# Expert results added into x by float32 products with zeros and ones, instead of a scatter to DRAM and a reload

## The reference

```python
def run_block(args):
    tok, e, wt = args
    xb = h[tok]
    y = (jax.nn.silu(xb @ w_g[e]) * (xb @ w_u[e])) @ w_d[e]
    return y.astype(jnp.float32) * wt[:, None]

ys = lax.map(run_block, (row_tok..., block_e, row_w...))
out = jnp.zeros((T, D), jnp.float32).at[row_tok].add(ys.reshape(P, D))
...
x = x_mid + g2 * f[:B * N].reshape(B, N, D)
return rmsnorm(x, final_norm)
```

## Time and profile before

| | us |
|---|---|
| runs | 1578.85, 1578.13, 1573.48 |
| median | 1578.13 |
| the profiled execution | 1576.79 |
| its span, first to last instruction | 1575.0 |
| TensorE busy | 1398.2 (89%) |
| VectorE busy | 724.6 (46%) |
| ScalarE busy | 415.5 (26%) |
| mean granted TensorE clock | 0.962 |

### The profile page before, as it was taken

How to read it: one execution, slowest core, us unless ns; L and a number is a source line. 1 busy time by engine, 2 the same in 40 slices (tenths; PEclk the granted TensorE clock), 3 DMA queues, 4 the chain that set the end, 5 groups by cost and what they waited for, 6 DMA issues and landing times.

```text
span 1575.0 us, 16738 instructions
## 1 busy us (share of the span) xinstructions
PE 1398.2 (89%) x6766; PEld 964.7 (61%) x6766; DVE 724.6 (46%) x1190; ACT 415.5 (26%) x585; POOL 49.1 (3%) x78
## 2 busy tenths in 40 slices
PE   6999999999949998778889785999896999999995
PEld 5889778787833432223233223788675888888883
DVE  5899977767322110001001004767668425343346
ACT  4522234463320000000000003423325314132323
POOL 0000000000000000100000100000000000000000
PEclk9999999999979999999999998999997999999997
DMA  9341343443678999999999997331011332332301
GB/s 368 116 161 54 127 160 134 163 163 98 276 298 343 426 426 428 426 426 427 427 426 426 426 415 258 101 121 54 28 53 54 107 107 82 105 103 83 107 0 54
DMA packets 116708, 336.88 MB, mean 214 GB/s; under 512 B 6824, under 2 KB 74536, under 8 KB 91168
## 3 DMA queue, kind: packets, MB, share of 16 engines
q1 hardware_dynamic: 109488, 316.82, 51.5%
q0 software_dynamic: 6576, 17.01, 3.0%
q10 hardware_dynamic: 576, 2.10, 0.3%
HBM read 331.42 MB, written 13.13 MB: 219 GB/s over the span
## 4 chain that ended last, share of the span: by engine, by line
PE 41%; SPq 18%; DMA 6%; DVE 5%; issue 1%; ACT 1%; ACTq 0%; DVEq 0%; POOLq 0%
SPq L1350 17%; PE second_bank L2504 10%; PE second_bank L2505 9%; PE second_bank L2506 9%; PE moe_bank L1704 5%; PE moe_bank L1716 3%; DMA moe_weights<-in_w_exp_down_dram 2%; DMA vals<-in_w_exp_down_dram 2%; PE second_bank L2638 1%; PE second_bank L2613 1%; DMA kq<-y_dram 1%; DVE x_mid L2417 1%; DMA work<-h_rows_dram,moe_tok_i 1%; DVE x_mid L2420 0%; PE second_bank L2621 0%
## 5 line engine op out<-in xcount | busy, mean ns | idle before, releaser
L1704 PE MATMUL moe_bank<-moe_weights,work 128*64 128x512 f32 x528 | 128.7, 639 | 35.6 <-DMA moe_weights<-in_w_exp_up_dram 22.5
L2504 PE MATMUL second_bank<-second_cx_lo,second_c_hi 128*128 128x512 f32 x352 | 140.2, 398 | 13.2 <-DVE second_cx_lo L2175 9.9
L1621 DVE TENSOR_TENSOR work<-moe_bank,work 128x512 f32<-128x512 f32 x17 | 11.8, 692 | 295.2 <-PE moe_bank L1704 295.2
L2505 PE MATMUL second_bank<-second_cx_hi,second_c_lo 128*128 128x512 f32 x352 | 138.1, 392 | 0.0
L2506 PE MATMUL second_bank<-second_cx_hi,second_c_hi 128*128 128x512 f32 x352 | 138.0, 392 | 0.0
L978 PE MATMUL mixer_bank<-mixer_h_lo,mixer_w_hi 128*128 128x512 f32 x320 | 131.8, 412 | 0.7 <-DVE mixer_w_lo L611 0.4
L2504 PE MATMUL second_bank<-g_lo,second_c_hi 128*128 128x512 f32 x320 | 127.9, 400 | 1.2 <-DVE g_lo L2322 1.2
L979 PE MATMUL mixer_bank<-mixer_h_hi,mixer_w_lo 128*128 128x512 f32 x320 | 126.6, 396 | 0.0
L980 PE MATMUL mixer_bank<-mixer_h_hi,mixer_w_hi 128*128 128x512 f32 x320 | 126.5, 395 | 0.0
L2505 PE MATMUL second_bank<-g_hi,second_c_lo 128*128 128x512 f32 x320 | 125.1, 391 | 0.0
L2506 PE MATMUL second_bank<-g_hi,second_c_hi 128*128 128x512 f32 x320 | 125.0, 391 | 0.0
(11 more groups left out here) (421 smaller groups left out, 2264.2 us busy)
## 6 DMA issues: line engine op xcount, KB each, us to landing
moe_weights<-in_w_exp_down_dram SPq DMA_DIRECT2D x20, 2048.0 KB, 33.6
moe_weights<-in_w_exp_gate_dram SPq DMA_DIRECT2D x17, 2048.0 KB, 33.2
moe_weights<-in_w_exp_up_dram SPq DMA_DIRECT2D x16, 2048.0 KB, 33.5
second_c_raw<-in_w_mlp_dram SPq DMA_DIRECT2D x32, 1024.0 KB, 5.0
mixer_raw<-in_w_in_dram SPq DMA_DIRECT2D x18, 1024.0 KB, 5.3
mixer_raw<-in_w_mod_t_dram SPq DMA_DIRECT2D x16, 1024.0 KB, 4.8
spare<-in_w_exp_up_dram SPq DMA_DIRECT2D x6, 2048.0 KB, 32.6
kq<-in_w_exp_down_dram SPq DMA_DIRECT2D x6, 2048.0 KB, 33.3
```

The lines of the kernel that those rows point to most:

```text
L1704: ins = pe.matmul(out[m * e:m * e + m, :], x_t[:, c, m * e:m * e + m], parts[:, e, k, :], start=(c == 0), stop=(c == KC - 1))
L2504: pe.matmul(out, a_hi, b_lo, start=first, stop=False)
L2505: pe.matmul(out, a_lo, b_hi, start=False, stop=False)
```

## The change

The scatter, the DRAM tensor `y`, its reload, and the gating, adding and transposing at the head of the second stage are removed. In their place:

- ScalarE and VectorE multiply a pair's result by the gate of each slot while they copy it into `y_rows`.
- VectorE writes for each pair a matrix of 128 slots by 512 tokens, one where a slot holds a token (`token_one`, from `iota_row`, now 512 wide).
- TensorE multiplies, for each of the 8 chunks of 128 features, `y_rows` (128 slots by 128 features) with `token_one`: 8 products of 128 x 128 by 128 x 512 (`results`), unsplit float32. They stand between parts 1 and 2 of the next pair; those of the last pair stand at the end. They go through banks 0, 1, 4 and 5.
- VectorE adds each of the 8 outputs, times `g2`, into `x_mid` (`added`).
- The gates are computed at the start of the stage, and two small lists bring them to the slots (`gate_list`, `slot_gates`, and the late ones with `late_list`).
- Six instead of four weight slots are filled from the mixer stage. Slot 4 is the memory of the mixer's `raw` buffers and is filled once the last low part is made; slot 5 is that of `w_hi[0]` and `w_lo[0]` and is filled when the last unit but one of the mixer is computed.
- GpSimd clears `x_rows` once before the first gather.

```diff
-EARLY = 4
+EARLY = 6
...
             sp.wait_ge(mlo_done, KC)
             for n in range(EARLY):
+                if n == 4:
+                    sp.wait_ge(lo_done, NS)
+                if n == 5:
+                    sp.wait_ge(acc_ready, first_tile[NS - 1])
                 first_experts(n)
...
-            sp.wait_ge(scattered, 16 * n_late + 16 * BLOCKS + 16)
-            for t in range(TC):
-                for k, rows in enumerate((vals, kq)):
-                    sp.dma_start(rows[:, 1024 * t:1024 * t + 1024],
-                                 dram["y"][...]).then_inc(y_landed[t], 16)
...
+            pool.wait_ge(xst_ready, 2 * TC)
+            step(pool.memset(x_rows, 0.0))
             pool.wait_ge(h2_stored, 16 * TC)
             pool.wait_ge(first_rows_ready, 1)
             gather_rows(tok_i[:, 0:1])
...
-                pool.wait_ge(y_low, b + 1)
-                pool.wait_ge(y_high, b + 1)
-                scatter_rows(row_i[:, b:b + 1])
...
-                act_e.wait_ge(scattered, 16 * no + 16)
-                act_e.activation(y_rows[:, 0:512], bank[6][:], ACT.Copy).then_inc(y_low, 1)
+                if at[1] is not None:
+                    act_e.wait_ge(late_columns, at[1] + 1)
+                elif at[0] == 0:
+                    act_e.wait_ge(slot_gates_ready, 1)
+                if at[1] is not None or at[0]:
+                    act_e.wait_ge(f_ready, 8 * no)
+                act_e.activation(y_rows[:, 0:512], bank[6][:], ACT.Identity, scale=gate_column(at)).then_inc(y_first, 1)
...
-            def y_second(at):
+            def second_half(at):
                 dve.wait_ge(*done(at, 5))
-                dve.wait_ge(scattered, 16 * turn_no(at) + 16)
-                dve.tensor_copy(y_rows[:, 512:1024], bank[7][:]).then_inc(y_high, 1)
+                dve.tensor_scalar(y_rows[:, 512:1024], bank[7][:], gate_column(at), None, ALU.mult).then_inc(y_second, 1)
+
+            def added(no):
+                if not isinstance(no, int) or no:
+                    dve.wait_ge(f_used, 8 * no)
+                for c in range(KC):
+                    dve.wait_ge(f_ready, 8 * no + (c + 1))
+                    dve.scalar_tensor_tensor(out=x_mid[:, c, :], in0=bank[F_BANK[c % 4]][:],
+                                             scalar=mod_col[:, 40 + c:41 + c], in1=x_mid[:, c, :],
+                                             op0=ALU.mult, op1=ALU.add).then_inc(f_used, 1)
+
+            def chosen_tokens(at):
+                dve.tensor_scalar(token_one, iota_row[:], token_column(at), None, ALU.is_equal).then_inc(one_ready, 1)
...
             for b in range(BEFORE):
+                if b == 2:
+                    late_lists()
+                if b:
+                    added(b - 1)
+                chosen_tokens((b, None, None))
                 if b == 1:
                     late_slots()
                 gated((b, None, None))
                 if b + 1 < BEFORE:
                     x_shifted((b + 1, None, None))
-                if b == 2:
-                    late_lists()
-                    token_gates()
-                y_second((b, None, None))
+                if b == 0:
+                    slot_gates()
+                second_half((b, None, None))
...
+            def results(no):
+                pe.wait_ge(y_first, no + 1)
+                pe.wait_ge(y_second, no + 1)
+                pe.wait_ge(one_ready, no + 1)
+                for c in range(KC):
+                    if c >= 4:
+                        pe.wait_ge(f_used, 8 * no + (c - 3))
+                    out = bank[F_BANK[c % 4]][:]
+                    pe.matmul(out, y_rows[:, 128 * c:128 * c + 128], token_one, start=True, stop=True)\
+                      .then_inc(f_ready, 1)
...
                     if j < 2:
                         pe.wait_ge(x_done, 2 * no + (j + 1))
+                    if j == 2 and (i is not None or b):
+                        ...
+                        results(b - 1 if i is None and n_late is None else ...)
                     if j == 4:
+                        if i is not None or b:
+                            pe.wait_ge(f_used, 8 * no)
                         before_down()
                         pe.wait_ge(a_done, no + 1)
-                        if i is not None or b:
-                            pe.wait_ge(y_low, no)
-                            pe.wait_ge(y_high, no)
...
                     transpose_act((b, None, None))
+                    if b == 0:
+                        gate_list()
                     if b == 1:
                         late_list()
...
+            results(n_late + (BLOCKS - 1))
...
             act.wait_ge(in_landed, 16)
             act.activation(w_hi[0][:], first_raw, ACT.Copy).then_inc(hi_done, 1)
-            for t in range(TC):
-                act.wait_ge(y_landed[t], 32)
-                act.activation(f_rows[:, t, :], f_rows[:, t, :], ACT.Identity, scale=gates[:, t, 0:1])\
-                   .then_inc(f0_ready, 1)
-            act.wait_ge(side_landed, 32)
-            act.activation(wf_hi[:], w_forget[:], ACT.Copy).then_inc(wfhi_done, 1)
             for c in range(KC):
-                act.wait_ge(xf_ready, c + 1)
                 act.activation(x_hi[:, c, :], x[:, c, :], ACT.Identity, scale=vec["final_norm"][:, c:c + 1])\
                    .then_inc(xhi_done, 1)
                 act.activation(sq[:, c, :], x[:, c, :], ACT.Square).then_inc(sq_ready, 1)
+            act.wait_ge(side_landed, 32)
+            act.activation(wf_hi[:], w_forget[:], ACT.Copy).then_inc(wfhi_done, 1)
             first_hi(1)
```

More of the change, by code:

```diff
@@ L69, in mixer_stage @@
         ident, ones = cst["ident"], cst["ones"]
-        raw = [sb(f"raw{i}", [P, 2048]) for i in range(2)]
-        w_hi = [sb(f"w_hi{i}", [P, 2048], F32R) for i in range(2)]
-        w_lo = [sb(f"w_lo{i}", [P, 2048], F32R) for i in range(2)]
+        raw = [stream[:, 2048 * i:2048 * i + 2048] for i in range(2)]
+        w_hi = [halves[0], sb("w_hi1", [P, 2048], F32R)]
+        w_lo = [halves[1], sb("w_lo1", [P, 2048], F32R)]
         h_hi = sb("h_hi", [P, KC, SEQ], F32R)
@@ L1205, in moe_stage @@
         ident, ones = cst["ident"], cst["ones"]
-        gates = cst["gates"]
-        slots = expert_slots(spare, work, vals, kq) + [sb(f"weights{i}", [P, 4096])[:] for i in range(SLOTS - EARLY)]
-        x_rows, y_rows = work[:, 4096:5120], work[:, 5120:6144]
+        slots = expert_slots(spare, work, vals, kq, stream, split) + \
+            [sb(f"weights{i}", [P, 4096])[:] for i in range(SLOTS - EARLY)]
+        x_rows = work[:, 4096:5120]
+        y_rows = work[:, 5120:6144]
+        token_one = vals[:, 4096:4608]
         act, silu_g = work[:, 6144:6656], work[:, 6656:7168]
@@ L1552, in _ @@
                .then_inc(first_rows_ready, 1)
[L1553 removed]
+            dve.tensor_scalar(tok_f[:, 0:BLOCKS], bank[3][:, 0:BLOCKS], 1024.0, None, ALU.add)
             def late_blocks():
@@ L1786, in second_stage @@
         bank = [ctx.enter_context(nc.psum_tensor(f"second_bank{i}", [P, 512], F32)) for i in range(8)]
-        ident, ones, gates = cst["ident"], cst["ones"], cst["gates"]
+        ident, ones = cst["ident"], cst["ones"]
         RAWC, SPC = 4, 2
@@ L2755, in build_program @@
             spare = two_stages.enter_context(nc.sbuf_tensor("spare", [P, 8448], F32))
-            used = mixer_stage(nc, cst, x_mid, mod_col, cols, work, g_hi, g_lo, vals, kq, spare, route, w, dram, two_stages,
-                               moe_sems, landed)
-            moe_stage(nc, cst, work, vals, kq, spare, landed, route, w, dram, moe_sems, used, y_landed, in_landed)
-        second_stage(nc, cst, x_mid, mod_col, vec, work, g_hi, g_lo, vals, kq, y_landed, in_landed, w, dram, out)
+            stream = two_stages.enter_context(nc.sbuf_tensor("stream", [P, 4096], F32))
+            with nc.sbuf_tensor("split", [P, 4096], F32) as split:
+                pass
+            halves = [two_stages.enter_context(nc.sbuf_tensor(f"split{i}", [P, 2048], F32R)) for i in range(2)]
+            used = mixer_stage(nc, cst, x_mid, mod_col, cols, work, g_hi, g_lo, vals, kq, spare, stream, split, halves,
+                               route, w, dram, two_stages, moe_sems, landed)
+            moe_stage(nc, cst, x_mid, mod_col, work, vals, kq, spare, stream, split, landed, route, w,
+                      dram, moe_sems, used, in_landed)
+        second_stage(nc, cst, x_mid, mod_col, vec, work, g_hi, g_lo, vals, kq, in_landed, w, dram, out)
 def columns(a):
```

191 lines of the change are left out of this document (95 added, 96 removed).

## The result

| | before | after |
|---|---|---|
| median of the runs, us | 1577.18 | 1603.45 |
| lowest to highest | 1573.48 to 1578.85 | 1602.25 to 1605.25 |
| the profiled execution | 1576.79 | 1605.25 |
| its span | 1575.0 | 1603.0 |
| ratio of the times, 95% interval | | 1.0161 (1.0142 to 1.0181) |

The changed kernel is 26.3 us slower by the medians, and 28.0 us by the two spans. The forecast was 1591.0 in a range of 1580 to 1609: right in its sign and inside its range, 12.5 us too low. The kernels of the experiments ran four times each, `e5_double` and the last two once; one run of `e8_split_rows`, at a granted clock of 0.737, took 2656.67 us and is left out of that kernel's median and ratio.

The account below looks back on a forecast made before the run. DMA was taken to bound the expert stage before and TensorE after; +32.0 for the stage, −8.0 for its start and −10.0 for the seam make +14.0 us on 1576.8, forecast as 1591, range 1580 to 1609.

Parts of the forecast that it names:

- What bounds before, and who bounds after: Expert stage: DMA bounds before at 31.1 us a pair; TensorE bounds after, 30.1 against DMA's 30.3; chance 0.77.
- the head start: Expert stage: with nine slots full at the start, DMA brings some 15 pairs (455 us) while TensorE computes 17 blocks (512 us).
- The group, 6.95 us: Eight results' products added to each block on TensorE, 6.95 us a group, bounds 6.87 to 7.6; sixteen make 111.2 us.
- TensorE's idle time of 80.2 and the +32.0 of the stage: Expert stage: 80.2 us of weight waits absorb added work; 111.2 + 1.0 − 80.2 puts its end 32.0 us later.
- The start, −8.0: Expert stage's start: early transfers let the gather go 5.5 us sooner and land 2.5 us faster; 8 us gained (5.5 to 12).
- the prediction's own sign: Expert stage's start: the forecast is wrong if the first pair starts outside 464 to 471.
- The seam, −10.0: Last product of the expert stage to the second stage's second unit: 26.1 us instead of 36.1, a gain of 10.0 (8 to 12).
- The mixer stage, put at zero: Mixer stage before the expert stage: the sum has no term for any change in its time.
- The additions pace the products: Rival, expert stage: VectorE's additions with their signals lengthen each group; at 8.5 us a group 1616 us; chance 0.08.
- DMA stays the bound: Rival, expert stage: a group well under 6 us, such as 3.5, leaves DMA the bound; 1540 us; chance 0.07.
- the prediction's point of balance: Expert stage: the sum of gains and losses is zero at 6.1 us a group.
- The Trainium skill's rule: Optimise the engine with the highest occupancy first: DMA, which the change relieves, so the expert stage would get shorter.

Follow-up runs that it names:

- e5_double: Changed kernel with every results' product issued twice, the second overwriting the first; 1722.35 us in one run.
- the last two: The changed kernel and the kernel before, each as it is, run and profiled once more; 1600.66 us and 1580.57 us.
- e8_split_rows: `e1_split` with slots 6 and 7 issued only behind the last evacuation of h's rows; 1566.47 us, ratio to before 0.9912.
- e7_rowsfirst: Changed kernel with the transfers into slots 6 to 8 held back until the first gather has landed; 1594.09 us, ratio to before 1.0089.
- e1_split: Changed kernel with each results' product as two fp32r products (high part and rest) instead of one unsplit float32; 1568.06 us, ratio to before 0.9926.
- e6_nosum: Changed kernel without the results' products and their additions, so x lacks the experts' results; 1551.87 us, ratio to before 0.9825.
- e2_half: Changed kernel with the results' products and additions over the first 256 tokens only; 1559.05 us, ratio to before 0.9872.
- e3_noscatter: Kernel before without its scatter, the reloads reading h's rows, so the experts' results are left out; 1559.97 us, ratio to before 0.989.

## Why the prediction was right in its sign and low in its size

- **What bounds before, and who bounds after.** Right. DMA bounds before, TensorE after: no waits for weights in the middle pairs, 0.37 us for an issue into slot 0, and +117 us in `e5_double` for doubled products. That the two are nearly equal in a steady pair (30.1 and 30.3 forecast, 30.33 measured by TensorE and 30.80 by DMA with this layout) and that the head start decides was right too.
- **The group, 6.95 us.** This is a mis-sized term. The form and its price were read rightly: 0.858 a product, the lower bound, in `e5_double`. But the group is 7.06, and with the broken seams of its neighbours 30.33 − 23.12 = 7.21, inside the bounds of 6.87 to 7.6. Sixteen groups make 4 us more than forecast. The late block's rows gave the inside of a group, not its two seams with half-array products.
- **TensorE's idle time of 80.2 and the +32.0 of the stage.** The sum held: 36.1 measured, of which 4 are the groups'. But not all of the 80.2 were waits for weights, as the prediction has it. The waits for weights that the profile lists behind the first product are 57 us; most of the rest is TensorE running slower after them. The mean granted clock of the earlier trace rows is 0.95 and 0.91, and in the kernel before the two parts behind a wait of 3.04 us take 9.9 us, with the clock at 0.50 from 610.5 to 615, where two parts take 6.87. With the idle time filled the clock is 1.00, and both are won back. The prediction took its blocks from stretches at full clock, so its sum had this in it without naming it; that was luck more than reading.

```profile
610.49 10.00 PE L1704 MATMUL moe_bank<-moe_weights,work 128*64 128x512 f32 x32 [3.04 <-DMA moe_weights<-in_w_exp_up_dram]
620.42 1.15 PE L1686 MATMUL moe_bank<-ident,work 128*128 128x128 f32 x8
```

- **The start, −8.0.** This step failed: −4.1 in one pair of profiles and −4.9 by the second look at each kernel, under the bound of 5.5. Two terms in it. The gather was to go 17.7 us after the stage's start and went after 19.7. The first 8.2 us were as forecast: 269 GB/s there are 2.2 MB, of 2.0 to 2.3. The other 4.1 MB then moved at 394 GB/s and not at 426 (10.4 us; the rate falls at the end, to 326 GB/s from 463 to 466), SyncE's next transfer, which waits for the rows too, goes 0.3 us later, and the gather 0.8 behind that. The forecast had nothing for the last two. And the gather was to take 6 and took 475.28 − 467.13 = 8.1 us, hardly less than the 8.6 of the earlier trace rows, with only one weight transfer beside it. `e7_rowsfirst` shows what a gather beside nothing takes: 4.5. By the prediction's own sign this was to be seen: the first product comes at 477.2, or 472.1 without the mixer stage's delay, outside its 464 to 471.
- **The seam, −10.0.** Right: −9.5 from the last down product to the first product of the second stage's second unit (1019.70 here). That is with a product step of 0.43 us in its first 3 us (1008.21 to 1008.64, at a granted clock of 0.51), which was 0.23 in before at a clock of 1.00.
- **The mixer stage, put at zero.** +5.1 in the profiled pair. No step of the prediction had it, and at least half of it isn't the change's, since 2.6 us vary in the kernel before alone; but the prediction held the mixer stage for a constant, and its end varies by up to 5 us, which the range should have had.
- **The rivals.** "The additions pace the products" is refuted for this kernel, and came true in `e1_split` for the last products of a group that fell to 4.28 us. "DMA stays the bound" was priced at 1540 for a group of 3.5: `e6_nosum`, with no group at all, needs 1552, so 1540 could not have been reached. The price had the old layout's 426 GB/s in it. Its condition was right, though: the prediction's point of balance was a group of 6.1 us, and with 4.28 the kernel is 11 us faster than before, as with 3.65 in `e2_half` (20 us faster). The Trainium skill's rule (Perfetto Trace Analysis, Identifying the Most-Contended Engine) is borne out by `e3_noscatter`, 19 us for relieving DMA alone; but what the change puts in the scatter's place, on the less busy engine, costs 43 us (from 1560.0 to 1603.5).

The miss in sum: +14 forecast behind the mixer stage; with groups +4 and start +3.5 it would have been 21.5, and 20.7 was measured. Of the other 5.6 us up to the 26.3 of the medians the two looks at each kernel show 3.2 in the mixer stage; the rest is within the runs' spread.

## What to carry to other kernels

Moving work from a busy DMA queue to a less busy engine pays up to the point where that engine's own time for a round meets the queue's; work that point out first (here 6.1 us a group by the prediction, between the 4.28 that came out faster and the 7.06 that came out slower), and then the format: the same sums as two fp32r products at 0.23 us each instead of one float32 product at 0.858 turned 1.6% slower into 0.7% faster. Where an engine bounds the stage, its first instruction is worth nearly its full time (9.1 us gave 8.4), and transfers that are issued early only because they can be are in the way of the one that it waits for. Where transfers bound the later pairs, as in `e8_split_rows`, 2.0 us at the start came through as well, but a gain of that size is lost in the spread of the times: look for it in the stage's own stretch.

## What the runs showed of the hardware that I had not expected

- A small gather (two of them move 0.44 MB) takes 4.5 us alone and 8.1 with a single 2 MB transfer issued 0.8 us ahead of it, though the mean share of DMA is then 0.76.
- In the changed kernels the transfers run at 419 to 420 GB/s and with the old layout at 426 to 427, in every profile in which DMA is full.
- The granted clock of the mixer stage falls in some executions under a full TensorE (0.66 in a window of 5 us), and with other falls that come and go it moves the end of an unchanged stage by up to 5 us.
- Waits for weights cost TensorE more than their length: behind one of 3.04 us the next two parts took 9.9 us instead of 6.87.
